# Column norms of the Hyena filters: GpSimd adds the row tiles' maxima and corrects row 0, and one matmul with all ones takes the place of the row-sum matmuls

## The reference

```python
h = (h @ w3 + b3).reshape(length, HY_ORDER, 2, HY_WIDTH)
h = h * jnp.exp(-t * deltas)[:, None, None, :]
fwd, bwd = h[:, :, 0], h[:, :, 1]
k = jnp.concatenate([fwd, jnp.zeros((1,) + fwd.shape[1:], f32), bwd[:0:-1]], axis=0)
k = k / jnp.sum(jnp.abs(k), axis=0, keepdims=True)
return jnp.fft.rfft(k, axis=0)
```

## Time and profile before

| what | value |
|---|---|
| median of three runs | 2343.63 us |
| span of the profiled execution, first to last instruction (its own time is given by this span alone) | 2341.4 us |
| PE busy | 2265.2 us (97%) |
| DVE busy | 1932.0 us (83%) |
| ACT busy | 1386.8 us (59%) |
| POOL busy | 322.8 us (14%) |
| stage prepare | from 0 to about 201 us |

### The profile page before, as it was taken

One profiled execution on the slowest core, in us unless ns is written; L12 is line 12 of the kernel. 1 busy time (PEld: TensorE's weight loads), 2 busy tenths in 40 slices (PEclk: granted clock), 3 DMA queues, 4 the chain that ended last, 5 costly groups with the idle time before them and its releaser, 6 DMA issues.

```text
span 2341.4 us, 28076 instructions
## 1 busy us (share of the span) xinstructions
PE 2265.2 (97%) x10776; PEld 1764.4 (75%) x10776; DVE 1932.0 (83%) x1344; ACT 1386.8 (59%) x956; POOL 322.8 (14%) x193
## 2 busy tenths in 40 slices
PE   7998999999999889999999999999999999999998
PEld 3346878875668568888888888888888888888886
DVE  6979798666965688988988889888888898898888
ACT  3135223242232466776777767768777677687777
POOL 1646000000000000120210201202102012021011
PEclk9999999999999889999999999999999999999999
DMA  6765445375733678999999999999999999999998
GB/s 239 300 255 202 126 125 154 88 300 210 257 128 117 257 293 323 410 356 390 388 360 411 363 373 411 355 390 390 358 412 362 372 410 356 387 393 357 414 364 345
DMA packets 204115, 731.66 MB, mean 312 GB/s; under 512 B 15491, under 2 KB 61483, under 8 KB 182999
## 3 DMA queue, kind: packets, MB, share of 16 engines
q1 hardware_dynamic: 196368, 701.90, 77.8%
q0 software_dynamic: 5328, 21.50, 3.2%
q10 hardware_dynamic: 2360, 7.47, 0.8%
HBM read 683.64 MB, written 47.17 MB: 312 GB/s over the span
## 4 chain that ended last, share of the span: by engine, by line
PE 69%; DVE 2%; issue 1%; ACT 0%; DMA 0%; POOL 0%; DVEq 0%; POOLq 0%; ACTq 0%
PE psum L2578 19%; PE psum L2552 10%; PE psum L2553 10%; PE psum L2554 10%; PE psum L2537 4%; PE psum L2538 4%; PE psum L2539 4%; PE psum L2521 2%; PE psum L2075 1%; PE psum L2110 1%; PE psum L2076 1%; PE psum L2077 1%; PE psum L2510 1%; DVE arena L2264 0%; DVE arena L2259 0%
## 5 line engine op out<-in xcount | busy, mean ns | idle before, releaser
L2680 DVE TENSOR_TENSOR w_low<-w_raw,w_high 128x4096 fp32r<-128x4096 f32 (+2 forms) x288 | 1162.6, 4063 | 69.6 <-ACT w_high L2600 67.2
L2600 ACT ACTIVATE w_high<-w_raw 128x4096 fp32r<-128x4096 f32 (+2 forms) x286 | 958.3, 3354 | 387.1 <-PE psum L2578 174.0
L2552 PE MATMUL psum<-w_high,x_high 128*128 128x512 f32 x1024 | 403.4, 394 | 0.0
L2554 PE MATMUL psum<-w_high,x_low 128*128 128x512 f32 x1024 | 398.8, 390 | 0.0
L2553 PE MATMUL psum<-w_low,x_high 128*128 128x512 f32 x1024 | 398.7, 389 | 0.0
L2552 PEld LDWEIGHTS psum<-w_high,x_high 128*128 128x128 f32 x1024 | 192.2, 188 | 43.8 <-DVE w_low L2680 5.2
L2554 PEld LDWEIGHTS psum<-w_high,x_low 128*128 128x128 f32 x1024 | 192.2, 188 | 40.5
L2553 PEld LDWEIGHTS psum<-w_low,x_high 128*128 128x128 f32 x1024 | 192.3, 188 | 38.2
L2578 PE MATMUL psum<-w_high,a_high 128*128 128x512 f32 x700 | 218.4, 393 | 0.0
L2578 PE MATMUL psum<-w_low,a_high 128*128 128x512 f32 x700 | 215.9, 390 | 0.0
L2578 PE MATMUL psum<-w_high,a_low 128*128 128x512 f32 x700 | 215.7, 389 | 0.0
(11 more groups left out here) (421 smaller groups left out, 3149.8 us busy)
## 6 DMA issues: line engine op xcount, KB each, us to landing
w_raw<-in_ex_w_gate SPq DMA_DIRECT2D x64, 2048.0 KB, 13.4
w_raw<-in_ex_w_up SPq DMA_DIRECT2D x64, 2048.0 KB, 14.9
w_raw<-in_ex_w_down SPq DMA_DIRECT2D x64, 2048.0 KB, 13.4
w_raw<-in_ex_w_gate SPq DMA_DIRECT2D x64, 768.0 KB, 4.5
w_raw<-in_ex_w_up SPq DMA_DIRECT2D x64, 768.0 KB, 6.0
w_raw<-in_ex_w_down SPq DMA_DIRECT2D x48, 1024.0 KB, 13.5
arena<-in_mod_w SPq DMA_DIRECT2D x16, 1024.0 KB, 6.8
arena<-in_mod_w SPq DMA_DIRECT2D x16, 512.0 KB, 8.4
```

What stands on the lines that cost most here:

```text
L2552: nc.tensor.matmul(o, xt_h[:, x], h[:, f], start=kk == 0, stop=False)
L2554: last = nc.tensor.matmul(o, xt_l[:, x], h[:, f], start=False, stop=kk == KD - 1)
L2600: nc.scalar.activation(high[n % NHI][:, 0:w], raw[n % NS][:, 0:w], ACT.Copy).then_inc(hi_done, 1)
L2680: nc.vector.tensor_tensor(low[n % NS][:, 0:w], raw[n % NS][:, 0:w], high[n % NHI][:, 0:w].bitcast(F32), ALU.subtract).then_inc(lo_done, 1)
```

## The change

GpSimd gets a new piece, column_norms(order): once tile 0 is multiplied, it corrects row 0 (a subtraction, a multiplication by 0.5, one by -1), and then it adds each tile's maximum to acc as it comes (a copy for the first). It stands before table 0 for order 0 and between tables 1 and 2 for order 1. TensorE's row_sums, ScalarE's total, VectorE's three instructions and sel go. column_sums multiplies acc, now a full 128x512 tile of partial sums, with the 128x128 matrix of ones. A buffer of ab comes free by GpSimd's addition and not by TensorE's matmul; TensorE's first step of an order waits for edge; the constants' semaphore counts to 5 and not to 9.

```diff
@@ gpsimd
-            for g in range(4):
-                nc.gpsimd.memset(sel[32 * g:32 * g + 1, :], 1.0).then_inc(ready, 1)
-                pool.wait_ge(ready, 5 + g)
...
+            def column_norms(order):
+                pool.wait_ge(kf, 8 * order + 1)
+                first = [sd[0:1, w, 0, :] for w in range(2)]
+                link(nc.gpsimd.tensor_tensor(first[0], first[0], first[1], ALU.subtract))
+                link(nc.gpsimd.tensor_scalar(first[0], first[0], 0.5, None, ALU.mult))
+                nc.gpsimd.tensor_scalar(first[1], first[0], -1.0, None, ALU.mult).then_inc(edge, 1)
+                if order:
+                    pool.wait_ge(amm, order)
+                for j in range(8):
+                    n = 8 * order + j
+                    pool.wait_ge(largest_of, n + 1)
+                    larger = ab[j % 3][:, 0, :]
+                    if j == 0:
+                        nc.gpsimd.tensor_copy(acc, larger).then_inc(summed, 1)
+                    else:
+                        nc.gpsimd.tensor_tensor(acc, acc, larger, ALU.add).then_inc(summed, 1)
+                    pool.wait_ge(summed, n + 1)
+
+            column_norms(0)
             pool.wait_ge(bbd, 1)
             for q in range(4):
+                if q == 2:
+                    column_norms(1)
                 tables(q)
@@ tensor
-            def row_sums(order, j):
...
             def column_sums(order):
-                pe.wait_ge(accd, order + 1)
+                pe.wait_ge(summed, 8 * order + 8)
                 pe.wait_ge(kf, 8 * order + 8)
-                last = nc.tensor.matmul(ps[:, 6, :], sel, acc, start=True, stop=True)
+                last = nc.tensor.matmul(ps[:, 6, :], k.ones, acc, start=True, stop=True)
...
                 kernel_rows(0, j)
-                if j in (3, 5, 7):
-                    row_sums(0, j - 3)
-                    row_sums(0, j - 2)
...
             pe.wait_ge(kf, 8)
+            pe.wait_ge(edge, 1)
             step(0)
-            row_sums(0, 6)
-            row_sums(0, 7)
...
@@ scalar
-            def total(order):
-                act.wait_ge(summed, 8 * order + 8)
-                nc.scalar.activation(acc, ps[:, 5, :], ACT.Copy).then_inc(accd, 1)
@@ vector
                 tt(sd[:, 1, j, :], ps[:, b + 1, :], decay[:, j, :], ALU.mult).then_inc(kf, 1)
-                if j == 0:
-                    dve.wait_ge(kf, n + 1)
-                    link(ts(acc[0:1, :], sd[0:1, 1, 0, :], 0.5, None, ALU.mult))
-                    link(stt(sd[0:1, 0, 0, :], sd[0:1, 0, 0, :], 0.5, acc[0:1, :], ALU.mult, ALU.subtract))
-                    ts(sd[0:1, 1, 0, :], sd[0:1, 0, 0, :], -1.0, None, ALU.mult).then_inc(edge, 1)
```

More of the change, by code:

```diff
@@ L228, in prepare @@
     silu_c = k.at(136, 1).rearrange("p (k m) -> p k m", k=KD)
-    sel = k.at(137, 1)[:, 0:P]
     acc = k.at(138, 2)
@@ L259, in prepare @@
     hid_hi, hid_lo, both_hi, both_lo = (k.sem("a_" + n) for n in ("hidhi", "hidlo", "bothhi", "bothlo"))
-    used, ev, tr, rowput, kload, kmm, kf, absd, summed, asum, accd, amm, afree, sdr, own, pown, hybin = (
-        k.sem("a_" + n) for n in ("used", "ev", "tr", "rowput", "kload", "kmm", "kf", "abs", "summed", "asum", "acc", "amm", "afree", "sd", "own", "pown", "hyb"))
+    used, ev, tr, rowput, kload, kmm, kf, absd, summed, amm, afree, sdr, own, pown, hybin = (
+        k.sem("a_" + n) for n in ("used", "ev", "tr", "rowput", "kload", "kmm", "kf", "abs", "summed", "amm", "afree", "sd", "own", "pown", "hyb"))
     aready, adone, cn, otd, epd, bdd, str_, lmm, sev, put_out = (
@@ L312, in bias @@
                 if c4 == 1:
-                    sp.wait_ge(ready, 9)
+                    sp.wait_ge(ready, 5)
                 else:
@@ L477, in kernel_rows @@
                 last.then_inc(kmm, 1)
-            def row_sums(order, j):
[L480 to L484, removed]
             def column_sums(order):
-                pe.wait_ge(accd, order + 1)
+                pe.wait_ge(summed, 8 * order + 8)
                 pe.wait_ge(kf, 8 * order + 8)
-                last = nc.tensor.matmul(ps[:, 6, :], sel, acc, start=True, stop=True)
+                last = nc.tensor.matmul(ps[:, 6, :], k.ones, acc, start=True, stop=True)
                 if order:
                     for q in range(HQ):
-                        last = nc.tensor.matmul(ps[:, 7, q:q + 1], acc[:, q * P:(q + 1) * P], sel[:, 0:1], start=True, stop=True)
+                        last = nc.tensor.matmul(ps[:, 7, q:q + 1], acc[:, q * P:(q + 1) * P], k.ones[:, 0:1], start=True, stop=True)
                 last.then_inc(amm, 1)
@@ L556, in _ @@
             pe.wait_ge(silu, 1)
-            pe.wait_ge(ready, 9)
+            pe.wait_ge(ready, 5)
             unit(0)
@@ L612, in _ @@
                 kernel_rows(1, j)
-                if j in (3, 5, 7):
-                    row_sums(1, j - 3)
-                    row_sums(1, j - 2)
                 if j in (1, 3, 5):
@@ L619, in _ @@
             pe.wait_ge(kf, 16)
+            pe.wait_ge(edge, 2)
             pe.wait_ge(colsd, 3)
             step(12)
-            row_sums(1, 6)
-            row_sums(1, 7)
             step(13)
@@ L741, in _ @@
             half_of(0)
-            total(0)
             act.wait_ge(used, 8)
@@ L755, in _ @@
             half_of(12)
-            total(1)
             act.wait_ge(ev, 3)
-            act.wait_ge(accd, 2)
             squares(0)
```

## The result

The changed kernel takes 2359.38 us (median of four runs, 2355.52 to 2359.42) where the kernel before takes 2344.27 beside it: ratio 1.0059, 95% interval [1.0047, 1.0071]. So it is slower, as forecast, but by 15 us and not by 5.9. The profiled execution is the one of 2355.52 (span 2353.8, 12.4 more than before). The stage mix starts at 214.63 in place of 201.90, 12.7 later, and what follows keeps that shift: in this execution the loss is made in prepare. The median of the four runs lies 3.9 above it; experiment 6 shows where a run of that length loses them.

A forecast was written before the change was run, and what follows sets the result against it. The prediction took VectorE's chain in prepare to delay TensorE, which is fully busy later and passes the delay to the end. 2343.63 + 2.9 (edge) + 2.2 (additions) + 0.8 (order 1) gave 2349.5 us, range 2343.5 to 2353.5.

The forecast's parts named there:

- The chain: In prepare, VectorE's lateness delays TensorE at quarter 0 and, through the states tables, quarter 2; the shift reaches the end.
- The edge: Order 0, GpSimd's three instructions correcting row 0: 4.58 us, making the chain 2.9 us late.
- rival (a): Row 0's correction is cheap on GpSimd, scalings near VectorE's 0.42 us: 2.4 us in all, time 2347.3; chance 0.17.
- Rival (b): Order 1, quarter 2: VectorE's states tables are not doubled and TensorE's 2.9 us gain stays, time 2345.8; chance 0.13.
- The additions of order 0: GpSimd's eight adds: 0.7 us for each beside VectorE's work from SBUF, half if partly overlapped; 2.2 us in all.
- The five meetings that I named: Order 0 additions beside phase arithmetic (j = 3), products (j = 6), before the last maximum, beside the factors, and first copy.
- (c): GpSimd's additions fully block VectorE, or tables 3 come late by a slow landing: 2352 to 2353 us; chance 0.15.
- Order 1: Tables 2, pushed behind the additions, slow VectorE's states tables; quarter 2 starts 0.8 us late, not 2.9 early.
- rival (d): TensorE pauses between tiles and its clock falls to 1.2 GHz around step 0: 2349.5 to 2351 us; chance 0.05.
- The sum: Edge 2.9, additions of order 0 2.2 and order 1 0.8 make 5.9 us over 2343.63: 2349.5 us.

The follow-up runs named there:

- experiment 6: The changed kernel run again, nothing altered, beside three others on the same chip: 2358.16 us, ratio 1.0057; profiled run 2359.13.
- experiment 3: The changed kernel without the arithmetic of GpSimd's tables 2, transfer and signals kept: 2351.28 us, ratio 1.0030 to the kernel before.
- experiment 4: The changed kernel with dummy matmuls in TensorE's pauses: 2357.44 us, ratio 1.0054; with fewer dummies 2356.39, 1.0044.
- experiment 5: The changed kernel with unit 21 moved behind tile 5, units 22 and 23 behind tile 7: 2355.63 us, 1.0041; same move in the kernel before: 2345.20, 1.0000.
- experiment 1: Parts of the change against the kernel before: order 0 alone 2351.82 us, order 1 alone 2350.38, additions alone 2354.50, edge alone 2354.52.

## Why the prediction was wrong

**What held.** The chain: VectorE in order 0, the states table in order 1, and a shift that passes on whole to the end. The edge: 4.46 us for 4.58 forecast, and 2.9 late as forecast beyond the later start; VectorE stands idle 4.39 us ahead of its first maximum. That one partition isn't cheaper, and that a scaling costs more than an addition, hold in the rows (1.48 and 1.51 against 1.29), so rival (a) falls. Rival (b) falls too: the halves are doubled.

**The additions of order 0: 2.2 forecast, 4.3 measured.** The step that failed is the price of 0.7 us for an exposed addition, taken from maxima beside the tables, and half of it for one partly beside. The rows after show waiting to the other's end. The five meetings that I named were the right ones: for 0.7, 0.7, 0.35, 0.35 and 0.1 they cost 0.96, 1.08, 0.75, 0.93 and 0.39, which is 4.1. The trace of the kernel before showed it too, in the instruction that lost 0.97:

```profile
124.37 1.34 POOL L292 TENSOR_TENSOR arena<-arena 128x512 f32<-128x512 f32 x1
...
124.61 1.65 DVE L802 SCALAR_TENSOR_TENSOR arena<-arena 1x512 f32<-1x512 f32 x1
```

It started 0.24 us into GpSimd's instruction and ended 0.55 after it. The Trainium skill (SBUF — State Buffer, section "SBUF: two separate sides") has the rule: the port pair that VectorE and GpSimd share is an exclusive lock, and the one that comes second fully blocks. The trace agrees with it; even a 128x32 instruction waited. I gave that case, (c), 0.15. Products that read PSUM keep 0.67 to 0.69, as forecast.

**Order 1: 0.8 forecast, 4.9 measured.** The kind of cost was right: without the tables' arithmetic it is gone (experiment 3). Its size was off in two places, which make up the 4.1 that are missing. The first half of the states table takes 9.25 us and not 7.6, 1.6 more: the last addition runs into it and GpSimd's table beside it from end to end. The 7.75 of the earlier trace rows was read ahead of quarter 1, where two of the six instructions met nothing or little (0.68 and 1.09). And this half starts at 155.26, which less the shift of 7.7 is 147.6, 2.5 later than the forecast 145.1. About 0.9 of that is the last maximum, 1.60 us for 0.69: it met an addition, and the sum leaves the additions of order 1 at nothing without a reason. The rest are the tiles, which were to end 1.9 us earlier and did not: the last maximum starts 57.6 us after quarter 0 (95.78 to 153.41), before 57.9. I removed TensorE's row sums and looked at VectorE's wait behind them, but not at what TensorE would wait for instead. It was the weights of unit 21, 5.28 us, and after them 1.2 GHz in tile 4: VectorE waited 1.52 there. Filling that wait or moving the unit gave back 1.7 to 1.8 up to quarter 2 (experiments 4 and 5).

**The clock, rival (d).** It fell as described there, and I gave it 0.05. But in order 0 it cost next to nothing (experiment 4), since VectorE was later still. In order 1, where (d) didn't look, the pause at unit 21 and the clock after it cost some 1.7 us together, and no run takes them apart. The chance was too low; that the price of up to 1.5 is near this is luck, since the place was another.

**The sum.** 0.4 start + 2.9 + 4.3 + 4.9 is 12.5, and mix starts 12.7 late; forecast 5.9. The terms describe this kernel only: taken out one at a time they don't give back these amounts (experiment 1). Some 2 to 3 us of the median more come from behind the start of mix, where no step of mine looked, and their cause stays open. My range ended at the case in which one term went badly; here the additions and order 1 both did, since a large part of both has one cause, more work on GpSimd beside VectorE, and I had treated their sizes as apart.

## What to carry to other kernels

Work that is moved to GpSimd is paid for on VectorE wherever that reads and writes SBUF alone: count each meeting as a wait to the end of GpSimd's instruction, in every place where the moved work falls, and count the work that is pushed back behind it as well. When work is taken from an engine, ask what it waits for next (here a transfer that the row sums had covered) and what its clock does after that pause. Undoing one part of a change doesn't price that part when another engine then becomes the late one. Costs with one cause go wrong together, so the range must hold them together.

## What the runs showed of the hardware

A GpSimd addition of one column took 0.19 us (median of 14) and one of 512 columns 1.27, but 1x512 took 1.29: here the columns count, the partitions don't. When VectorE and GpSimd both worked from SBUF, instruction after instruction (156 to 164 us in the changed kernel), they took turns: each started one every 1.47 us, where alone VectorE's take 0.68 and GpSimd's 1.06. TensorE's granted clock was 0.68 in the 8 us around the restart from a pause of 5.54 us (its matmuls then came every 0.43 us in place of 0.23), and 1.00 throughout with dummy matmuls in the same pause.
